# First attention's last head: 48 products of the output projection between its steps, and the places and engines of the work around them

## The chip, the cores and the metric

One core of one Trainium2 chip runs the whole program. The core has five engines with a program each: TensorE (PE, matrix products and transposes), VectorE (DVE), ScalarE (ACT), GpSimd (POOL), and SyncE (SP), whose queue starts the transfers between device memory and the core's memory. An engine takes its instructions strictly in order and waits at one until the semaphores named in the code have reached their counts. The metric is the time of one execution on the device in microseconds (us); lower is better.

## The reference

Two layers on an input of 1024 rows by 1024 columns, all in float32, so the sums must be good to float32. Layer 0 is differential attention and an MLP; layer 1 is a sliding window attention and an MLP. The change is at the end of layer 0's attention:

```python
h = rms_norm(x, attn_norm_g[0])
q, k, v = h @ w_qkv                       # 8 heads; q and k in two halves of 64, v of 128
p = softmax(q_c @ k_c.T - slope*distance) # for c = 0 and 1, chunk-causal mask
o = (p[0] - lam * p[1]) @ v               # one 1024x128 block for each head
o = rms_norm(o, subln_g) * (1 - lambda_init)
x = x + concat(o of 8 heads) @ w_o        # w_o: 1024x1024
x = x + relu(rms_norm(x, mlp_norm_g[0]) @ w_up)**2 @ w_down
```

## The kernel before

**Numbers.** A float32 value is held as a high part (rounded by ScalarE with a copy) and a low part (VectorE: value minus high part, the function `low`). A product of two such values is three matrix products: high by high, high by low, low by high. For a block of the attention's output these parts are `a_hi[:, c]` and `a_lo[:, c]`, c being the head (a "chunk" of 128 rows of w_o), each 128 partitions by 1024. A panel of w_o is 128 of its columns, with its parts `w_hi[i]` and `w_lo[i]`, which lie in the memory of `w_op`; so the traces call them w_op.

**The attention.** Heads run in a pipeline over 8 blocks of queries (steps s = 0 to 7). For each step TensorE makes the scores, VectorE takes their maxima (`maxima`, `both_maxima`), ScalarE the exponentials (`exps`), VectorE mixes the two softmaxes (`mix`), TensorE transposes the mixed weights (`transpose_weights`), ScalarE and VectorE split them (`high_wT`, `low_wT`), and TensorE multiplies them with the values (`values`, one step behind). In heads 0 to 6 the projection of the next head's q, k and v fills TensorE between these steps. The last head (head 7, `last_head` on each engine) has no next head: its steps hold only its own scores, transposes and values.

A head's output is divided by its root mean square ("norm"): VectorE makes a first guess of the inverse root from the sums of squares (`o_factors`), three Newton steps refine it, a product applies it to the head's block, and TensorE transposes the result (`transpose_outputs`). ScalarE copies that out (`evac_o`, to `xT`, called oT here) and makes `a_hi` (`high_early`), VectorE `a_lo`. For heads 0 to 6 the Newton steps and the product are GpSimd's (its `head`, lines 866 to 884: 13 small instructions and one of 128x1024). For head 7 they are VectorE's, `rsqrt_steps_dve` and the product, right behind the last values.

**The output projection.** It follows in `segment(0)` of each engine. Eight panels, two halves of 512 rows each, in three pairs of PSUM banks in turn, `wo_bank[0]`: score0 and score1 hold two banks each, and proj and pv one each. A panel is 8 chunks by 2 halves by 3 = 48 products of 128x512. Panels 0 and 1 begin early: behind the last values TensorE makes their products with `a_hi` of chunks 0 to 6, then those with `a_lo`, and transposes the outputs of head 7 between them. VectorE adds each half to the residual (`add_x`, result `xs`), which needs the residual's tile, loaded from device memory by SyncE (`load_unit`: four tiles of 128x512 for each two panels, a "unit"). ScalarE multiplies `xs` with the norm's gain and squares it, GpSimd sums the squares (`ss`) and makes sums and differences of the unit's tiles for the MLP (`minus`), which uses seven products of sub-blocks for each eight. VectorE splits the units' seven operands (`xop`). A panel's weights are loaded by SyncE (`load_wo`, two places `w_raw` in the memory of `w_quad`), and split by ScalarE and VectorE (`split_panel`), panels 0 and 1 in the last head's steps 5 and 6, panel 2 behind head 7's norm, and each later one two panels ahead, in the loop of the segment. SyncE loads the second unit only when `a_lo` of all eight chunks is there.

**The order of work** is written out by hand, engine by engine. No planner and no cost table takes part: each engine's instructions run in the order in which the functions write them.

## Time and profile before

| | |
|---|---|
| time, median of 3 runs | 2198.53 us (2195.86 to 2199.34) |
| the profiled execution's own time | 2196.21 us |
| its span in the trace | 2194.5 us |
| granted TensorE clock, mean of the span | 0.991 of full speed |
| TensorE busy | 2143.5 us, 98% of the span, 11580 products and transposes |
| VectorE busy | 1566.1 us, 71% |
| ScalarE busy | 1137.7 us, 52% |
| GpSimd busy | 761.1 us, 35% |
| chain that ended last, by engine | PE 82%, DVE 10%, issue 4%, ACT 2% |

The time is that of the whole execution on the device; the span is the stretch that the trace covers, 1.7 us shorter. Busy is the time in which an engine ran an instruction. The clock is the share of its full speed that TensorE was granted. The stretch that the change touches is short: the last head from 469.8 to 518.0 us, the projection's eight panels from there to 606.

### The profile page before, as it was taken

To read this page: it belongs to the slowest core of one execution; us is meant where nothing else is said; L and a number is where in the kernel's file an instruction comes from. 1 tells how busy PE (TensorE), PEld (TensorE's weight loads), DVE (VectorE), ACT (ScalarE), POOL (GpSimd) and SP (SyncE) were. 2 spreads that over 40 slices of the span, in tenths; PEclk is the share of its full clock that TensorE was granted. 3 is DMA by queue.
4 is the path that set the end of the run, shared out by engine and by line. 5 is a ranking of instruction groups with operands and counts; after the bars stand their busy time and mean duration, and the time that the engine had idled before them with its cause. 6 is when DMAs were issued, how large, how long until landed. Compare 5 with 4: busy or idle time off the path is not lost.

```text
span 2194.5 us, 34725 instructions
## 1 busy us (share of the span) xinstructions
PE 2143.5 (98%) x11580; PEld 1843.0 (84%) x11580; DVE 1566.1 (71%) x3011; ACT 1137.7 (52%) x2429; POOL 761.1 (35%) x1200
## 2 busy tenths in 40 slices
PE   7999999998999999999999999999999999999999
PEld 6999999987888888788888899988888888788887
DVE  6788788887586666778767757775766666886783
ACT  5566566655455455624434446764555555443342
POOL 3334333331642222333225225435622222322331
PEclk9999999989999999999999999999999999999999
DMA  6111110003424444754534111105244445654252
GB/s 207 42 30 30 29 29 23 1 20 106 135 87 158 158 158 143 262 185 164 192 131 157 62 53 48 29 11 173 92 158 158 152 141 209 251 192 151 99 184 84
DMA packets 190916, 257.71 MB, mean 117 GB/s; under 512 B 15136, under 2 KB 139552, under 8 KB 186144
## 3 DMA queue, kind: packets, MB, share of 16 engines
q1 hardware_dynamic: 190752, 255.65, 35.0%
q8 instruction: 87, 1.43, 0.3%
q14 instruction: 77, 0.63, 0.1%
HBM read 174.09 MB, written 79.69 MB: 116 GB/s over the span
## 4 chain that ended last, share of the span: by engine, by line
PE 82%; DVE 10%; issue 4%; ACT 2%; POOLq 0%; DVEq 0%; DMA 0%; POOL 0%; ACTq 0%; SPq 0%
PE score L2193 42%; PE proj L2193 15%; PE trb L2193 14%; PE pv L2193 6%; DVE xop L1548 4%; DVE w_op L1548 2%; DVE xT L1868 1%; PE trb L2236 1%; ACT p L1119 1%; PE trb L2290 1%; PE trb L2611 1%; DVE p L1735 0%; PE score L2598 0%; DMA xop<-u_dram 0%; PE trb L2264 0%
## 5 line engine op out<-in xcount | busy, mean ns | idle before, releaser
L2193 PE MATMUL score<-xop,w_op 128*128 128x512 f32 x3840 | 892.5, 391 | 6.5 <-DVE xT L1868 5.7
L2193 PEld LDWEIGHTS score<-xop,w_op 128*128 128x128 f32 x3840 | 723.4, 189 | 160.4 <-issue 10.2
L2193 PE MATMUL trb<-xop,w_op 128*128 128x512 f32 x1536 | 362.0, 391 | 5.3 <-DVE xT L1868 4.6
L897 POOL TENSOR_TENSOR w_quad<-w_quad,w_sum 128x512 f32<-128x512 f32 x64 | 83.7, 1308 | 782.6 <-DVE w_op L1548 782.6
L2193 PEld LDWEIGHTS trb<-xop,w_op 128*128 128x128 f32 x1536 | 287.5, 188 | 68.7 <-DVE w_op L1548 7.4
L1041 ACT ACTIVATE w_op<-w_quad 128x512 fp32r<-128x512 f32 (+1 forms) x336 | 214.0, 644 | 228.1 <-PE score L2193 109.3
L1548 DVE TENSOR_TENSOR w_op<-w_quad,w_op 128x512 fp32r<-128x512 f32 (+1 forms) x335 | 293.1, 880 | 41.0 <-ACT w_op L1041 41.0
L1868 DVE TENSOR_TENSOR xT<-score,xT 128x512 f32<-128x512 f32 x160 | 109.0, 686 | 138.8 <-PE score L2193 133.1
L1548 DVE TENSOR_TENSOR xop<-xop 128x1024 fp32r<-128x1024 f32 x112 | 150.9, 1365 | 3.7 <-ACT xop L1041 3.7
L1041 ACT ACTIVATE quad<-score 128x512 f32<-128x512 f32 x96 | 57.2, 596 | 176.4 <-PE score L2193 174.1
L1041 ACT ACTIVATE xop<-xop 128x1024 fp32r<-128x1024 f32 x112 | 117.0, 1053 | 56.1 <-DMA xop<-u_dram 55.2
L2193 PE MATMUL proj<-wa_hi,a_hi 128*128 128x384 f32 x418 | 142.5, 341 | 0.9 <-DVE v_parts L1549 0.9
L1119 ACT ACTIVATE p<-p,nm_a,slopes 128x128 f32<-128x128 f32 (+7 forms) x112 | 96.4, 863 | 90.3 <-DVE nm_a L1740 90.3
L2193 PE MATMUL proj<-wa_hi,a_lo 128*128 128x384 f32 x418 | 139.9, 335 | 0.0
L2193 PE MATMUL proj<-wa_lo,a_hi 128*128 128x384 f32 x418 | 139.8, 334 | 0.0
L1868 DVE TENSOR_TENSOR quad<-trb,quad 128x512 f32<-128x512 f32 x64 | 44.2, 690 | 110.1 <-PE trb L2193 75.3
L1041 ACT ACTIVATE w_op<-w_sum 128x512 fp32r<-128x512 f32 x128 | 76.9, 625 | 81.1 <-PE trb L2193 33.2
L2193 PE MATMUL score<-a_hi,w_op 128*128 128x512 f32 x368 | 110.3, 391 | 0.1
L519 POOL TENSOR_TENSOR chain_p<-rstd_qk 128x8 f32<-128x8 f32 x96 | 19.1, 199 | 244.6 <-DVE rstd_qk L511 235.3
L897 POOL TENSOR_TENSOR w_quad<-w_quad 128x512 f32<-128x512 f32 x64 | 100.6, 1573 | 5.0
L1735 DVE CUSTOM_DVE_ANT_0 p<-score,dist_a 128x128 f32<-128x128 f32 (+7 forms) x112 | 80.3, 754 | 29.8 <-PE score L2193 29.8
L911 POOL TENSOR_TENSOR w_sum<-w_quad 128x512 f32<-128x512 f32 x64 | 89.2, 1394 | 31.2 <-DMA w_quad<-in_mlp_w_down 24.1
(320 smaller groups left out, 4285.4 us busy)
## 6 DMA issues: line engine op xcount, KB each, us to landing
xop<-u_dram SPq DMA_DIRECT2D x112, 512.0 KB, 5.0
u_dram<-quad SPq DMA_DIRECT2D x32, 1536.0 KB, 9.5
w_quad<-in_mlp_w_up SPq DMA_DIRECT2D x64, 512.0 KB, 5.4
w_quad<-in_mlp_w_down SPq DMA_DIRECT2D x64, 512.0 KB, 4.9
wa_raw<-in_a_w_qkv SPq DMA_DIRECT2D x96, 128.0 KB, 2.5
quad<-xT_dram SPq DMA_DIRECT2D x32, 256.0 KB, 3.8
xT_dram<-xs SPq DMA_DIRECT2D x32, 256.0 KB, 2.4
u_dram<-quad SPq DMA_DIRECT2D x32, 256.0 KB, 3.5
```

Of the source, the lines that this page charges most:

```text
L519: eng.tensor_tensor(t, out, out, ALU.mult)
L897: return pool.tensor_tensor(out, x, y, ALU.subtract)
L911: pool.tensor_tensor(w_full(n, "S1"), quarter(n, 1, 0), quarter(n, 1, 1), ALU.add)\
L1041: return nc.scalar.activation(out, in_, ACT.Copy, scale=scale)
L1119: nc.scalar.activation(p[:, 0:keys], p[:, 0:keys], ACT.Exp, bias=nm_a[i][:, c:c + 1], scale=one(slopes, h), accum_out=ssum[par][:, c, s:s ...
L1548: return nc.vector.tensor_tensor(out, full, hi.bitcast(F32), ALU.subtract)
L1735: nc.vector.tensor_tensor_reduce(out=p[:, 0:keys], in0=score[c][:, 0:keys], in1=dist_a[:, S - keys:S], scale=1.0, scalar=LOWEST, op0=ALU.a ...
L1868: return nc.vector.tensor_tensor(out, a, b, ALU.add)
L2193: return nc.tensor.matmul(out, a, b, start=start, stop=stop, **kw)
L2236: last = nc.tensor.transpose(trb[b][:, P * (kc - 4 * i):P * (kc - 4 * i + 1)], p0[block_s % 2][:, P * kc:P * (kc + 1)], ident[:, :])
L2290: last = nc.tensor.transpose(trb[b][:, P * i:P * (i + 1)], qk2[:, (s - 3) % 4 + i % 2, P * (i // 2):P * (i // 2 + 1)], ident[:, :])
L2611: last = nc.tensor.transpose(trb[b][0:P - lo, P * u:P * (u + 1)], pb[:, e, r, lo:P], ident[:, :])
```

## The change

Eight parts, in the order of the program.

1. The panels are split in the order 2, 0, 1, 3 and so on (`SPLIT_ORDER`). Panel 2's weights get a place of their own (`raw2`), are loaded behind the attention's own last weights and split in head 6, step 2. Panel 0's high part is made after the last head's first exponentials, its low part moves from VectorE to GpSimd, in four pieces of 128x256. Panel 3 gets a place of its own (`w_op` slot 4 and `w_low3`) and is split right behind the last head.
2. `a_hi` of chunks 0 to 3 is made at the last head's start, of 4 and 5 in step 1.
3. TensorE makes 36 products of `a_hi` of chunks 0 to 5 with both parts of the weights (`panel_high`) between the steps of the last head, into the bank proj, which the attention no longer uses: 12 each for panel 2's second half, panel 0's first and panel 0's second. ScalarE copies each finished sum out (`keep`, to `kept`, 128x512). 12 more, panel 2's first half, stand behind the last transposes and ahead of the last values, in the bank where they stay.
4. GpSimd adds the three kept sums to the residual's tiles before VectorE adds the rest: two when the norm is done, and the third behind `clear()`, when the second unit is loaded and ahead of its first difference and sums of squares. `add_x` waits for these three.
5. Behind the last values TensorE makes 24 products of panel 1, 12 of chunk 6 for three panels, 18 with `a_lo` of chunks 0 to 2, the transposes of head 7, and 24 with `a_lo` of chunks 3 to 6; then chunk 7 of the three panels (18) and panel 3.
6. The norm of head 7 moves from VectorE to GpSimd, its product in four pieces of 128x256; head 6's product is in four pieces as well. VectorE makes `a_lo` of chunks 0 and 1 ahead of head 7's guess and the others behind it.
7. VectorE's guess for head 6 moves from step 2 to step 1, behind the maxima.
8. Some semaphores are merged (`lam_steps`, `passed`), with the same order of work.

```diff
+LATE = 6
+SPLIT_ORDER = (2, 0, 1, 3, 4, 5, 6, 7)
...
+        scope = ExitStack()
+        kept = [sb(f"kept{i}", [P, HALF], F32, scope) for i in range(3)]
...
+        raw2 = sb("raw2", [P, KC, P], F32, scope)
+        w_raw2 = raw2[:, :, :]
...
+        w_low3 = sb("w_low3", [P, KC, P], F32R, scope)
...
+            if i == 3 and not seg:
+                return w_op[:, 4, :, :].rearrange("p a (k n) -> p (a k) n", n=P), w_low3[:, :, :]
...
+        def split_count(seg, panel):
+
+            return KC * seg + (panel if seg else SPLIT_ORDER.index(panel)) + 1
...
+            sp.wait_ge(wa_lo_done, NH * 4)
+            sp.dma_start(w_raw2, w_out[0].rearrange("(k p) n -> p k n", p=P)[:, :, 2 * P:3 * P])\
+                .then_inc(w_in[0], 16)
...
                         sp.wait_ge(w_lo_done, KC * seg + i - 1)
+                    elif i == 3:
+                        sp.wait_ge(w_lo_done, split_count(0, 1))
...
-            run_heads(pool, head)
+            def norm_outputs(done, o):
+
+                pool.wait_ge(o_rstd, done)
+                norm_steps(rstd_o[:, :], chain_o, NB)
+                for b in range(0, NB, 2):
+                    last = pool.tensor_tensor(o[:, b:b + 2, :], o[:, b:b + 2, :],
+                                              rstd_o[:, b:b + 2].unsqueeze(2).to_broadcast([P, 2, P]), ALU.mult)
+                last.then_inc(o_normed, 1)
+
+            def last_head():
+
+                pool.wait_ge(w_lo_done, split_count(0, 2))
+                pool.wait_ge(w_hi_done, split_count(0, 0))
+                for k in range(0, KC, 2):
+                    last = pool.tensor_tensor(w_lo[0][:, k:k + 2, :], w_raw[0][:, k:k + 2, :],
+                                              w_hi[0][:, k:k + 2, :].bitcast(F32), ALU.subtract)
+                last.then_inc(w_lo_done, 1)
+                norm_outputs(NH - 1, head_out[0])
+                norm_outputs(NH, head_out[1])
+
...
+                    for i, (panel, half) in enumerate(((2, 1), (0, 0), (0, 1))):
+                        if panel:
+                            continue
+                        pool.wait_ge(half_kept, i + 1)
+                        pool.wait_ge(quad_in[0], 64)
+                        x = quad[0][:, TILE[0, half], :]
+                        pool.tensor_tensor(x, x, kept[i][:, :], ALU.add).then_inc(half_added, 1)
...
+                if seg == 0:
+                    pool.wait_ge(quad_in[1], 64)
+                    x = quad[1][:, TILE[0, 1], :]
+                    pool.tensor_tensor(x, x, kept[0][:, :], ALU.add).then_inc(half_added, 1)
...
+                act.wait_ge(w_in[i % 2], panel // 2 * 16 + (16 if panel else 32))
...
+                    act.wait_ge(mixed, NH * NB)
...
+                def keep(i):
+                    act.wait_ge(half_ready, i + 1)
+                    copy(kept[i][:, :], proj[:, :]).then_inc(half_kept, 1)
+
                 act.wait_ge(qkv_ready, NH * NB)
+                high_early(0)
+                high_early(1)
                 last_exps(0)
                 high_wT(uses, 0)
+                split_panel(0)
+                high_early(2)
...
                 for s in range(NB - 1):
 
...
                         act.drain()
                         square_outputs(h * 4, 1 - par, 6)
                     if s == 1:
-                        high_early(0)
...
                     if s == 2:
+                        keep(0)
...
-                    if s >= 4:
-                        high_early(s - 3)
+                    if s == 4:
+                        keep(1)
                     if s in (4, 5):
                         act.drain()
...
+                    if s == 5:
+                        split_panel(1)
+                    if s == 6:
+                        keep(2)
                 act.drain()
                 square_outputs(h * 4 + 3, par, 4)
...
+                        act.wait_ge(w_in[0], 16)
+                        copy(w_hi[2], w_raw2).then_inc(w_hi_done, 1)
...
+            split_panel(3)
...
                     if s == 0:
                         row_sums(h - 1, NB - 1)
-                    if s == 2:
-                        o_factors(h, 1 - par)
-                    if s == NB - 1:
-                        split_panel(0)
...
+                    if s == 1:
+                        o_factors(h, 1 - par)
...
+                dve.wait_ge(w_lo_done, split_count(0, 0))
                 split_panel(1)
...
+            low_outputs_a(0, 2)
             take_outputs(NH * NB - 1, 1, NB - 2)
             o_factors(NH, 1)
-            dve.wait_ge(o_normed, NH - 1)
-            dve.drain()
-            rsqrt_steps_dve(nc.vector, rstd_o[:, :], chain_o, chain_p, NB)
...
-            nc.vector.tensor_tensor(head_out[1], head_out[1],
...
+            low_outputs_a(2, EARLY[0])
+            split_panel(3)
...
+                        if seg == 0 and (i, half) in ((0, 0), (0, 1), (2, 1)):
+                            dve.wait_ge(half_added, i + half + 1 if i == 0 else 3)
...
+                pe.wait_ge(qkv_free, NH * NB)
+                pe.wait_ge(w_lo_done, split_count(0, 2))
+                panel_high(proj[:, :], 2, 1, (0, 1))
                 values(uses, 0, NB - 1, h * 4 - 1, 1 - par)
+                panel_high(proj[:, :], 2, 1, (2,))
...
+                    if s == 0:
+                        panel_high(proj[:, :], 2, 1, (3,))
+                    if s == 2:
+                        panel_high(proj[:, :], 2, 1, (4, 5)).then_inc(half_ready, 1)
+                    if s == 3:
+                        pe.wait_ge(half_kept, 1)
+                        pe.wait_ge(w_lo_done, split_count(0, 0))
+                        panel_high(proj[:, :], 0, 0, (0, 1, 2))
+                    if s == 4:
+                        panel_high(proj[:, :], 0, 0, (3, 4, 5)).then_inc(half_ready, 1)
+                    if s == 5:
+                        pe.wait_ge(half_kept, 2)
+                        panel_high(proj[:, :], 0, 1, (0, 1, 2))
+                    if s == 6:
+                        panel_high(proj[:, :], 0, 1, (3, 4, 5)).then_inc(half_ready, 1)
                     if s + 2 < NB:
...
+            pe.wait_ge(score_max, 2 * NH * NB)
+            pe.wait_ge(half_kept, 3)
+            panel_high(wo_bank[0][2][0], 2, 0, range(LATE))
             values(last_uses, 0, NB - 1, NH * 4 - 1, 1)
...
-                        x_h = a_hi[:, k, HALF * i:HALF * (i + 1)]
-                        mm(wo_bank[0][slot][i], w_hi[slot][:, k, :], x_h, k == 0, False)
-                        mm(wo_bank[0][slot][i], w_lo[slot][:, k, :], x_h, False, False)
-                    if slot and k == 2:
-                        transpose_outputs(last_uses, NH, 1)
-            for slot in range(2):
-                for k in range(EARLY[0]):
-                    pe.wait_ge(o_split, k + 1)
-                    for i in range(2):
-                        mm(wo_bank[0][slot][i], w_hi[slot][:, k, :], a_lo[:, k, HALF * i:HALF * (i + 1)], False, False)
+            pe.wait_ge(w_lo_done, split_count(0, 1))
+            for half in range(2):
+                panel_high(wo_bank[0][1][half], 1, half, range(LATE))
+            pe.wait_ge(pv_free, NH * 4)
+            for panel in range(3):
+                for half in range(2):
+                    panel_high(wo_bank[0][panel][half], panel, half, range(LATE, EARLY[0]))
+            for c in range(3):
+                panel_lows(c)
+            transpose_outputs(last_uses, NH, 1)
+            for c in range(3, EARLY[0]):
+                panel_lows(c)
```

`panel_high` and `panel_lows` are new and called above:

```diff
+            def panel_high(out, panel, half, chunks):
+
+                for c in chunks:
+                    pe.wait_ge(o_early_hi, c + 1)
+                    x_h = a_hi[:, c, HALF * half:HALF * (half + 1)]
+                    kept_half = (panel, half) in ((2, 1), (0, 0), (0, 1))
+                    mm(out, w_hi[panel][:, c, :], x_h, c == 0 or kept_half and c == LATE, False)
+                    last = mm(out, w_lo[panel][:, c, :], x_h, False, kept_half and c == LATE - 1)
+                return last
+
+            def panel_lows(c):
+
+                pe.wait_ge(o_split, c + 1)
+                for panel in range(3):
+                    for half in range(2):
+                        mm(wo_bank[0][panel][half], w_hi[panel][:, c, :], a_lo[:, c, HALF * half:HALF * (half + 1)], False, False)
```

**The order before and after.** First TensorE, from the values of the last head's step 5 to the segment. Names: p_0 and p_1 are the mixed weights of even and odd steps, ident is the identity of a transpose, oraw the output of head 7; score, proj and pv are PSUM banks. Before, in two pieces, around the last transposes and behind the last values:

```order
L2193 MATMUL pv<-v_parts,wT_lo 128x256
L2193 MATMUL pv<-v_parts,wT_hi 128x256
L2193 MATMUL pv<-v_parts,wT_lo 128x256
L2236 MATMUL trb<-ident,p_1 128x128 x8
L2193 MATMUL pv<-v_parts,wT_hi 128x256
L2193 MATMUL pv<-v_parts,wT_lo 128x256
L2193 MATMUL pv<-v_parts,wT_hi 128x256
```

```order
L2193 MATMUL pv<-v_parts,wT_hi 128x256
L2193 MATMUL pv<-v_parts,wT_lo 128x256
L2193 MATMUL score<-a_hi,w_op 128x512 x40
L2264 MATMUL trb<-ident,oraw 128x128 x8
L2193 MATMUL score<-a_hi,w_op 128x512 x16
L2193 MATMUL score<-a_lo,w_op 128x512 x28
L2193 MATMUL score<-a_hi,w_op 128x512
```

After, the same two places:

```order
L2266 MATMUL pv<-v_parts,wT_hi 128x256
L2266 MATMUL pv<-v_parts,wT_lo 128x256
L2309 MATMUL trb<-ident,p_1 128x128 x8
L2266 MATMUL proj<-a_hi,w_op 128x512 x12
L2266 MATMUL pv<-v_parts,wT_hi 128x256
L2266 MATMUL pv<-v_parts,wT_lo 128x256
```

```order
L2266 MATMUL score<-a_hi,w_op 128x512 x32
L2266 MATMUL proj<-a_hi,w_op 128x512 x2
L2266 MATMUL pv<-a_hi,w_op 128x512 x2
L2266 MATMUL score<-a_lo,w_op 128x512 x4
L2266 MATMUL proj<-a_lo,w_op 128x512
L2266 MATMUL pv<-a_lo,w_op 128x512
```

and, three rows of the same kind later:

```order
L2266 MATMUL score<-a_lo,w_op 128x512 x4
L2266 MATMUL proj<-a_lo,w_op 128x512
L2266 MATMUL pv<-a_lo,w_op 128x512
L2337 MATMUL trb<-ident,oraw 128x128 x8
L2266 MATMUL score<-a_lo,w_op 128x512 x4
```

Twelve products stand between the last transposes and the last values (the proj row of the first piece after); of the earlier steps, steps 0 and 2 to 6 have two, four or six there. Behind the last values the 40 products with `a_hi` ahead of the transposes of oraw have become 36, and 18 with `a_lo` have come in, so that 54 stand ahead of these transposes instead of 40.

VectorE behind the last values' split, before:

```order
L1548 TENSOR_TENSOR wT_lo<-trb,wT_hi 128x512 x2
L1822 TENSOR_REDUCE oraw<-pv 128x256
L1831 TENSOR_TENSOR s0sq<-ssum 128x8
L1832 TENSOR_SCALAR chain_o<-oss 128x8
L1834 SCALAR_TENSOR_TENSOR chain_o<-s0sq,chain_o 128x8
L509 TENSOR_SCALAR chain_s<-chain_o 128x8
L511 TENSOR_SCALAR rstd_o<-chain_s 128x8
L536 SCALAR_TENSOR_TENSOR chain_p<-chain_o,rstd_o 128x8
L538 TENSOR_TENSOR chain_p<-chain_p,rstd_o 128x8
```

And after:

```order
L1619 TENSOR_TENSOR a_lo<-xT,a_hi 128x1024 x2
L1895 TENSOR_REDUCE oraw<-pv 128x256
L1904 TENSOR_TENSOR s0sq<-ssum 128x8
L1905 TENSOR_SCALAR chain_o<-oss 128x8
L1907 SCALAR_TENSOR_TENSOR chain_o<-s0sq,chain_o 128x8
L529 TENSOR_SCALAR chain_s<-chain_o 128x8
L531 TENSOR_SCALAR rstd_o<-chain_s 128x8
L1619 TENSOR_TENSOR a_lo<-xT,a_hi 128x1024 x5
L1619 TENSOR_TENSOR w_low<-w_quad,w_op 128x1024
L1619 TENSOR_TENSOR a_lo<-xT,a_hi 128x1024
L1939 TENSOR_TENSOR xs<-score,quad 128x512 x4
L1619 TENSOR_TENSOR w_op<-w_quad,w_op 128x1024
```

The guess (the row L531, before L511) is no longer followed by the Newton steps (L536 to L540, three of each) and the product L1853; the splits of `a_lo` follow at once.

GpSimd, from head 6's product (`xT`) on. Before:

```order
L880 TENSOR_TENSOR xT<-xT,rstd_o 128x1024
L889 MEMSET ss 128x512 x2
L897 TENSOR_TENSOR quad<-quad 128x512
L894 TENSOR_TENSOR ss<-ss,quad 128x512 x4
L897 TENSOR_TENSOR quad<-quad 128x512 x4
```

After, from the end of head 7's Newton steps (their first 11 rows left out):

```order
L545 TENSOR_SCALAR chain_p<-chain_p 128x8
L547 TENSOR_TENSOR rstd_o<-rstd_o,chain_p 128x8
L912 TENSOR_TENSOR oraw<-oraw,rstd_o 128x256 x4
L949 TENSOR_TENSOR quad<-quad,kept 128x512 x2
L932 MEMSET ss 128x512 x2
L957 TENSOR_TENSOR quad<-quad,kept 128x512
L940 TENSOR_TENSOR quad<-quad 128x512
L937 TENSOR_TENSOR ss<-ss,quad 128x512 x4
L940 TENSOR_TENSOR quad<-quad 128x512 x4
```

Head 7's Newton steps and product, and the three additions of `kept`, now stand ahead of the first sum of the unit (`quad<-quad`) and of the squares (`ss<-ss,quad`).

## Rows read from the trace of the kernel before

**Rows 1.** Stretches: start:end, length, busy time (count) by engine, clock, DMA share, GB/s.

```profile
469.80:518.00 48.20, 34.88 (x218) 28.30 (x218) 39.41 (x107) 32.86 (x78) 9.11 (x28) 0.82 0.15 42
476.00:478.00 2.00, 1.88 (x10) 1.53 (x11) 1.88 (x8) 0.54 (x2) 1.15 (x6) 0.55 0.00 0
488.00:490.00 2.00, 2.00 (x12) 2.00 (x12) 1.93 (x7) 0.00 (x0) 1.90 (x1) 0.54 0.00 0
```

**Rows 2.** TensorE's waits in 469.8:518: who waited <- for whom, us in all, times, longest.

```profile
PE pv L2193 <- DVE wT_lo L1548: 8.0, 4, 3.6
PE score L2193 <- DVE mx_a L1775: 3.9, 4, 1.5
```

**Rows 3.** Timeline of TensorE: start, us, instruction, count, idle before it <- who ended it.

```profile
474.67 0.35 PE L2193 MATMUL pv<-v_parts,wT_hi 128*128 128x256 f32 x1 [2.15 <-DVE wT_lo L1548]
...
516.00 0.36 PE L2193 MATMUL pv<-v_parts,wT_hi 128*128 128x256 f32 x1 [1.67 <-DVE wT_lo L1548]
...
518.00 9.26 PE L2193 MATMUL score<-a_hi,w_op 128*128 128x512 f32 x40
527.10 1.03 PE L2264 MATMUL trb<-ident,oraw 128*128 128x128 f32 x8
```

**Rows 4.** Timeline of VectorE behind the last values.

```profile
520.47 0.17 DVE L511 TENSOR_SCALAR rstd_o<-chain_s 128x8 int32<-128x8 int32 x1
...
524.07 8.03 DVE L1548 TENSOR_TENSOR a_lo<-xT,a_hi 128x1024 fp32r<-128x1024 f32 x7
...
533.15 1.22 DVE L1548 TENSOR_TENSOR a_lo<-xT,a_hi 128x1024 fp32r<-128x1024 f32 x1
```

**Rows 5.** Timeline of GpSimd: head 6's Newton steps begin, and their product.

```profile
482.78 0.20 POOL L519 TENSOR_TENSOR chain_p<-rstd_o 128x8 f32<-128x8 f32 x1 [1.55 <-DVE rstd_o L511]
...
487.54 2.36 POOL L880 TENSOR_TENSOR xT<-xT,rstd_o 128x1024 f32<-128x1024 f32 x1
```

**Rows 6.** Timeline of VectorE at two places where GpSimd is busy.

```profile
39.43 1.23 DVE L1568 CUSTOM_DVE_ANT_0 x_junk<-x_tok 128x1024 f32<-128x1024 f32 x1
...
423.19 0.93 DVE L1749 SCALAR_TENSOR_TENSOR coef_a<-ssum,neg_lam,rcp_a 128x1 f32<-128x1 f32 x1
```

**Rows 7.** Timeline of GpSimd at the same two places.

```profile
39.51 1.21 POOL L523 TENSOR_TENSOR chain_p<-chain_p 128x8 f32<-128x8 f32 x1
...
423.06 1.05 POOL L873 TENSOR_TENSOR qk<-qk,rstd_qk 128x512 f32<-128x512 f32 x1
```

**Rows 8.** Timeline of ScalarE: head 7's output copied out and split; two squares.

```profile
527.73 1.27 ACT L1041 ACTIVATE xT<-trb,gsub 128x512 f32<-128x512 f32 x2 [6.22 <-PE trb L2264]
529.09 1.06 ACT L1041 ACTIVATE a_hi<-xT 128x1024 fp32r<-128x1024 f32 x1
...
547.41 1.14 ACT L1277 ACTIVATE quad<-xs 128x512 f32<-128x512 f32 x2
```

**Rows 9.** SyncE's loads of the second unit, and their landing.

```profile
535.38 2.32 SPq L670 DMA_DIRECT2D quad<-xT_dram  x4
...
DMA to landing us min/median/max: 5.6/5.9/7.4
```

**Rows 10.** Timeline of VectorE in the panels; last row GpSimd.

```profile
549.53 2.20 DVE L1548 TENSOR_TENSOR w_op<-w_quad,w_op 128x1024 fp32r<-128x1024 f32 x1 [2.78 <-ACT w_op L1041]
...
572.85 1.37 DVE L1868 TENSOR_TENSOR xs<-score,quad 128x512 f32<-128x512 f32 x2 [2.61 <-PE score L2193]
...
599.92 2.38 DVE L1548 TENSOR_TENSOR w_op<-w_sum,w_op 128x512 fp32r<-128x512 f32 x2
...
602.82 0.68 DVE L1868 TENSOR_TENSOR xs<-score,quad 128x512 f32<-128x512 f32 x1
604.82 3.07 DVE L1548 TENSOR_TENSOR xop<-quad,xop 128x512 fp32r<-128x512 f32 x2 [1.31 <-ACT xop L1041]
...
595.64 1.29 POOL L897 TENSOR_TENSOR w_sum<-w_sum,w_quad 128x512 f32<-128x512 f32 x1
```

**Rows 11.** Chain that ended last, the piece before the first MLP products.

```profile
584.37 24.53 PE score L2193 x108
```

## What the change will do to the time

> **What bounds the kernel now.** First the page's part 1: TensorE is busy 98% of the span, so on the whole only what shortens TensorE's own list or fills its gaps can help. Then the busy time by stretches: the last head is the exception. In its 48.20 us TensorE is busy 34.88, so 13.3 us are idle, and its mean clock is 0.82 [rows 1]. The waits say for whom: 8.0 us for VectorE's splits of the transposed weights ahead of the values, 3.9 us for maxima ahead of scores [rows 2]. The timeline shows where: a wait of 2.15 us ahead of 474.67, one of 1.67 us ahead of 516.00, one of 3.6 between [rows 2, 3]. Behind 518.00 TensorE has none: 40 products take until 527.10, 0.2275 us each (9.10/40) [rows 3]. Call the end of the last values T: 518.0 before. From there to the first MLP product all 384 products of the eight panels run on the critical chain; its last piece, 96 of them and 12 of the MLP, starts at 584.37 [rows 11], so the MLP begins at about 584.37 + 96 x 0.2275 = 606.2.
>
> The last view is VectorE in the panels. It is less idle than its 71% say. It splits panel 4 at 549.53 (call this D), waits 2.61 us for TensorE at 572.85, and makes the last half of panel 7 at 602.82; the first operand that is waited for in the MLP comes out of 604.82 [rows 10]. So a second chain, VectorE with ScalarE and GpSimd, runs just behind TensorE, and the saving is limited by the one that shrinks less.
>
> **TensorE's side.** 48 products leave the stretch behind T: 48 x 0.2275 = 10.9 us. Of these 36 go into the idle 13.3 us of the last head: at full clock 8.2 us of work, in groups of 2 to 6 (0.5 to 1.4 us), each ahead of values that wait for VectorE in any case. The last 12 take 2.73 us at full clock where 1.67 us of waiting stood [rows 3], so T moves by +1.06, to about 519.1. Below this: if the groups keep the clock up, the transposes and values at the end get quicker, and T may be 517.4. Above: 520 to 521, where ScalarE's three copies to `kept` (the nearest row is 0.6 us for a 128x512) or GpSimd's pieces hold VectorE. The extra copy and split in head 6 I cost at nothing, since there the projection of the next head keeps TensorE busy; without that cover they are 1.06 + 1.15 [rows 4, 8], an end of the range. If nothing else is late the saving is 10.9 − 1.1 = 9.8 us.
>
> **The chain behind T on the other engines** (times after T). VectorE's guess ends at 520.47 + 0.17 = T + 2.64 [rows 4]; the two splits ahead of it in the order lie under the last 12 products. Now the norm is GpSimd's. In head 6, 13 Newton steps there took 487.54 − 482.78 = 4.76 us, and the product 2.36 [rows 5]. VectorE had both done 3.43 us after its guess (524.07 − 520.64) [rows 4], T + 6.1; so even alone the move costs 3.7 us: norm at T + 9.8. But at once behind the guess VectorE makes seven splits of 1.15 us (8.03/7) [rows 4], each reading two operands, while GpSimd makes small steps. What then happens is in two places of the trace. A VectorE instruction of 1.23 us and a GpSimd step of 128x8, which took 0.20 [rows 5] elsewhere, overlap: GpSimd's takes 1.21. A GpSimd product of 1.05 us and a 128x1 of VectorE: VectorE's takes 0.93, ending with GpSimd's [rows 6, 7]. So the later one waits until the earlier has ended, in both directions. With every gap between splits used by one step, six steps cost 1.15 + 0.2 = 1.35 each, 8.1 us; the other seven 0.37 (4.76/13), 2.6; the product about 2.0: norm at 2.64 + 8.1 + 2.6 + 2.0 = T + 15.3. I take this, and 9.8 as the other end.
>
> The Trainium skill has this rule (SBUF — State Buffer, "Who interferes with whom"): a VectorE instruction with two inputs in SBUF and a GpSimd one that reads SBUF share a port pair under an exclusive lock, taken by whichever issues first, and the other fully blocks. The 1.21 against 0.20 agrees. A sharing of throughput instead of a lock would leave the norm near T + 9.8.
>
> TensorE reaches the transposes after 54 products, at T + 12.3 (before: after 40). It waits there 3.0 us, which only eats part of the 9.8. From transposes (527.10) to the end of `a_hi` (529.09 + 1.06) are 3.05 us [rows 3, 8], and the split 1.15: `a_lo` of chunk 7 at T + 19.5. SyncE issues the second unit's loads only behind that: from 534.37 (533.15 + 1.22) [rows 4] to the last issue, 535.38 + 2.32, are 3.3 us, and each lands 5.6 to 7.4 us after its issue [rows 9]: T + 28.4. Before, nothing early depended on it. Now GpSimd waits for it in order to add the third kept sum, and queued behind are its first difference and the squares of panel 0. ScalarE's squares of panel 1 write the tiles that these read, and behind them stands its copy for panel 4. So: addition 1.3 and difference 1.3 (as the 1.29 of 595.64 [rows 10]), two squares 2.5, ScalarE's square 0.57 (1.14/2) [rows 8], copy 1.06, handoffs 0.3: D = T + 28.4 + 7.0 = T + 35.4. Before D was T + 31.5. With T = 519.1, D = 554.5, 5.0 us later than before.
>
> **How much of that is hidden.** From D to 602.82 VectorE's chain has the 2.61 us wait for TensorE; at the end the GpSimd sums are ready at 596.93 and VectorE reads them at 599.92 with a copy of 0.6 and handoffs of 0.3 between, 2.1 us to spare. So the chain needs 53.3 − 4.7 = 48.6 us from D. The first MLP operand that VectorE makes late is ready at 605.5 (604.82 + 0.68) and is needed after six products, 606.2 + 1.4 = 607.6: another 2.0. Together 6.7 of cover against 5.0 lost: **saving 1.7 us**. The third addition in itself, the two others (TensorE still has panel 3 to do) and the merged semaphores add nothing more. Panel 3's split right behind the last head is made before D and so takes 2.2 us of ScalarE and VectorE from the loop; I count that as filling VectorE's wait, worth 0 to 1.
>
> **The sum.** The profiled execution took 2196.2 us of its own: 2196.2 − 1.7 = 2194.5. The median of the three runs is 2.3 above it: 2196.8. I predict 2196.5, as the small terms lean to the good side.
>
> **The rivals.**
> *A: GpSimd's norm is not held up.* For it: its steps are 0.20 us and VectorE's instructions have handoffs between them. Against: 1.21 us in rows 7. The norm is at T + 9.8, TensorE arrives at T + 12.3 without waiting, the chain is 3.0 us shorter, the saving 1.7 + 3.0 = 4.7: 2193.8.
> *B: TensorE bounds all through.* For it: 98% busy, and the chain shows only TensorE in rows 11. Then VectorE's margins are larger than I read them, or loads land sooner, and the whole 9.8 us come in, with up to 0.7 of gaps: 2198.5 − 10.5 = 2188.
> *C, slower: the last head's products run at half clock.* Behind the wait of 2.15 us the clock was 0.55 from 476 to 478 and still 0.54 at 488 to 490, and there TensorE was busy 94 to 100% [rows 1, 3]. A product at half clock costs 0.455 (twice 0.2275). If the clock stays low between 490 and 512 too, the 22 products of steps 2 to 5 take 10 us instead of 5, without cover, since all else of TensorE doubles as well; T = 519 + 5 + about 1 for VectorE's guess behind it = 524.5 to 525. D moves with it, 10.5 us later than before against 6.7 of cover: 4 slower, about 2202.5. It decides if the granted clock from 490 to 506 is nearer to 0.5 than to 1.0. Against it: the clock fell behind that wait, and the products shorten the waits.
>
> **Chances.** The forecast 0.48, its own range 2193.5 to 2199.5; A 0.18; B 0.20; C 0.14. Differences under 0.2% (4.4 us) can't be told from none: under 2194.1 is faster, over 2202.9 slower. B is all faster, A about half, the forecast 0.06 of its 0.48: 0.35. C is about half slower, and a little of the forecast: 0.13. The rest is 0.52. The range reaches from 2187 (B with T at 517.4) to 2202.5.
>
> **What would show it.** In the changed kernel's trace: T between 518 and 521; the last head's clock; GpSimd's steps for head 7 at over 1 us each next to VectorE's splits, and a wait of TensorE of about 3 us ahead of its transposes; GpSimd waiting for the second unit's load until T + 28 with ScalarE's copy for panel 4 waiting behind it; split of panel 4 at about 554.5; the MLP starting at about 604.5. A start of the MLP before 598 shows B; T over 523 shows C. I am wrong if VectorE's split of panel 4 is early and yet nothing is gained, or if TensorE waits in a place not named here.

## The result, and the profile after

The changed kernel is slower: 2202.14 us, median of 16 runs (2197.95 to 2203.74), against 2198.48 us for the kernel before (16 runs, 2195.41 to 2203.51). The ratio is 1.0014, 95% interval 1.0007 to 1.0020: 3.1 us lost, 1.5 to 4.4. That is under the 0.2% named in the prediction, and on the other side of what it forecast, 2 us faster.

The two traces have to be laid over each other first: the profiled execution of the changed kernel is the slowest of its sixteen (2203.74 us), that of the kernel before is on the fast side (2196.21). Their spans differ by 6.3 us, and the first 2.07 us of this are there before anything that the change touches: head 6's last seven transposes start at 462.63 in the kernel before and at 464.70 in the changed one. TensorE's timeline and the stretch of 44 to 47 us show where most of it, 1.6 us, comes from, the kernel before first:

```profile
43.71 0.65 PE L2290 MATMUL trb<-ident,qk 128*128 128x128 f32 x4 [2.26 <-POOL qk L873]
...
44.00:47.00 3.00, 3.00 (x21) 3.00 (x20) 2.81 (x9) 0.80 (x3) 0.00 (x0) 1.00 0.39 141
```

and the changed kernel, in the same place of the program:

```profile
44.08 0.34 PE L2363 MATMUL trb<-ident,qk 128*128 128x128 f32 x1 [2.25 <-POOL qk L896]
...
44.00:47.00 3.00, 2.92 (x11) 2.92 (x12) 2.89 (x8) 1.16 (x3) 0.02 (x1) 0.54 0.26 97
```

Both wait 2.25 us for the same norm; behind it one execution goes on at full clock and the other at 0.54 for three microseconds. The work is the same there. So I measure from T0, the start of those seven transposes, and write T, D and the rest against it.

| us after T0 | before | after |
|---|---|---|
| end of the last values, T | 55.4 | 58.2 |
| split of panel 4 on VectorE, D | 86.9 | 93.5 |
| MLP's seventh product on TensorE (first operand made late) | 144.7 | 146.7 |
| first sums of squares on TensorE | 154.3 | 159.5 |
| spread of the row factors on TensorE | 169.0 | 172.2 |

The sums of squares are TensorE's products of `ones` and `ss`, the spread its next products of `ss` and `ones`. The last line leaves 3.2 us, close to the 3.1 of the medians; from there to the end the two spans differ by another 1.0, which was not followed. (The seventh product before is 605.97 + 6 x 0.2275.) What TensorE waited for in the changed kernel, from the last head on (columns as in [rows 2]):

```profile
PE pv L2266 <- DVE wT_lo L1619: 5.4, 3, 2.2
PE score L2266 <- DVE xop L1619: 4.7, 1, 4.7
PE trb L2337 <- POOL oraw L912: 2.1, 1, 2.1
PE score L2266 <- DVE w_op L1619: 1.2, 1, 1.2
PE proj L2266 <- DVE w_op L1619: 1.1, 1, 1.1
...
PE score L2266 <- DVE mx_a L1849: 0.8, 1, 0.8
```

The waits of the last head have shrunk from 8.0 and 3.9 us to 5.4 and 0.8 [rows 2]: the products do fill them. But four waits of 9.1 us stand where there was none. TensorE's own list became 10.9 us shorter behind T (48 x 0.2275), and it waits for most of that. Its timeline at these places:

```profile
513.99 0.35 PE L2266 MATMUL pv<-v_parts,wT_hi 128*128 128x256 f32 x1 [2.18 <-DVE wT_lo L1619]
...
516.07 1.91 PE L2309 MATMUL trb<-ident,p 128*128 128x128 f32 x8
517.63 3.51 PE L2266 MATMUL proj<-a_hi,w_op 128*128 128x512 f32 x12
...
522.89 7.44 PE L2266 MATMUL score<-a_hi,w_op 128*128 128x512 f32 x32
...
537.44 1.10 PE L2337 MATMUL trb<-ident,oraw 128*128 128x128 f32 x8 [2.12 <-POOL oraw L912]
...
605.23 1.52 PE L2266 MATMUL score<-xop,w_op 128*128 128x512 f32 x6
611.42 3.34 PE L2266 MATMUL score<-xop,w_op 128*128 128x512 f32 x6 [4.67 <-DVE xop L1619]
614.55 4.38 PE L2266 MATMUL trb<-xop,w_op 128*128 128x512 f32 x12
```

The 54 products end 12.4 us behind 522.89, and the transposes of head 7 then wait 2.12 us. The MLP's first six products take 1.52 us; then comes the wait of 4.67 us, and behind it six take 3.34 and twelve 4.38 (twelve took 2.93 and twelve 2.91 before, from 605.97 on). The stretches show the clock there, and in the last head (columns as in [rows 1]):

```profile
469.80:522.90 53.10, 45.09 (x284) 36.09 (x283) 43.98 (x111) 37.60 (x89) 12.26 (x35) 0.90 0.11 31
...
488.00:490.00 2.00, 2.00 (x7) 1.22 (x5) 1.59 (x7) 1.53 (x4) 1.21 (x6) 0.50 0.01 4
516.00:518.00 2.00, 2.00 (x11) 2.00 (x10) 0.96 (x2) 0.60 (x1) 0.00 (x0) 0.50 0.02 6
612.00:614.00 2.00, 1.95 (x5) 1.13 (x4) 2.00 (x3) 0.58 (x2) 0.51 (x1) 0.50 0.00 0
```

TensorE is busy all or nearly all of 488 to 490, 516 to 518 and 612 to 614 and gets half of its clock, each time behind a wait of 2.2 to 4.7 us.

**The chain.** GpSimd's norm of head 7 and third addition, VectorE, and ScalarE ahead of panel 4:

```profile
525.62 1.11 POOL L539 TENSOR_TENSOR chain_p<-rstd_o 128x8 f32<-128x8 f32 x1 [31.93 <-DVE rstd_o L531]
...
531.41 1.00 POOL L539 TENSOR_TENSOR chain_p<-rstd_o 128x8 f32<-128x8 f32 x1
532.55 0.20 POOL L543 TENSOR_TENSOR chain_p<-chain_p 128x8 f32<-128x8 f32 x1
...
535.06 2.32 POOL L912 TENSOR_TENSOR oraw<-oraw,rstd_o 128x256 f32<-128x256 f32 x4
...
551.46 1.29 POOL L957 TENSOR_TENSOR quad<-quad,kept 128x512 f32<-128x512 f32 x1 [10.66 <-DMA quad<-xT_dram]
```

```profile
525.45 5.77 DVE L1619 TENSOR_TENSOR a_lo<-xT,a_hi 128x1024 fp32r<-128x1024 f32 x5
...
540.66 1.23 DVE L1619 TENSOR_TENSOR a_lo<-xT,a_hi 128x1024 fp32r<-128x1024 f32 x1 [8.30 <-ACT a_hi L1096]
...
552.26 1.37 DVE L1939 TENSOR_TENSOR xs<-score,quad 128x512 f32<-128x512 f32 x2 [6.17 <-DMA xT_dram<-xs]
558.16 1.93 DVE L1619 TENSOR_TENSOR w_op<-w_quad,w_op 128x1024 fp32r<-128x1024 f32 x1 [4.53 <-ACT w_op L1096]
...
610.01 3.04 DVE L1619 TENSOR_TENSOR xop<-quad,xop 128x512 fp32r<-128x512 f32 x2 [1.31 <-ACT xop L1096]
```

```profile
555.29 0.63 ACT L1348 ACTIVATE quad<-xs 128x512 f32<-128x512 f32 x1 [0.91 <-POOL ss L937]
...
557.08 1.04 ACT L1096 ACTIVATE w_op<-w_quad 128x1024 fp32r<-128x1024 f32 x1
```

GpSimd's first six steps take 0.7 to 1.2 us beside VectorE's six splits of 1.15, those behind them 0.20. The norm ends at 537.4, T + 14.5. GpSimd then waits for the second unit's load, adds the third kept sum at 551.46, and its difference and squares, for which ScalarE waits, come only behind that. D is 558.16, T + 35.3.

**The last head.** GpSimd's four pieces of panel 0 run from 483.26 to 486.05, and VectorE's guess for head 6, now in step 1, falls exactly there:

```profile
483.26 2.79 POOL L921 TENSOR_TENSOR w_op<-w_quad,w_op 128x256 fp32r<-128x256 f32 x4
```

```profile
483.44 0.58 DVE L1904 TENSOR_TENSOR s0sq<-ssum 128x8 f32<-128x8 f32 x1
...
485.48 0.61 DVE L531 TENSOR_SCALAR rstd_o<-chain_s 128x8 int32<-128x8 int32 x1
486.00 0.41 DVE L1619 TENSOR_TENSOR wT_lo<-trb,wT_hi 128x256 fp32r<-128x256 f32 x1
```

Its five instructions span 2.65 us; such a guess spanned about 1.0 in the kernel before (0.17 each [rows 4]). The split of the transposed weights (486.00) stands behind, and the third transposes are at T0 + 22.8 instead of 21.2. The last transposes are 1.1 us late (T0 + 51.4 instead of 50.2), T 2.8.

### The profile page after: what moved, and what is told of

The parts are those of the page before. It is cut to its first block and busy times, and to the rows that moved or that the text cites. A ratio compares the mean times of both kernels' runs of the same rounds, so it can differ in the third digit from the quotient of the medians.

```text
span 2200.8 us, 34754 instructions
## 1 busy us (share of the span) xinstructions
PE 2140.2 (97%) x11580; PEld 1836.8 (83%) x11580; DVE 1568.0 (71%) x3000; ACT 1138.7 (52%) x2432; POOL 780.3 (35%) x1227
## 5 line engine op out<-in xcount | busy, mean ns | idle before, releaser
L1096 ACT ACTIVATE quad<-score 128x512 f32<-128x512 f32 x96 | 57.2, 596 | 176.2 <-PE score L2266 173.8
L1096 ACT ACTIVATE xop<-xop 128x1024 fp32r<-128x1024 f32 x112 | 116.9, 1053 | 58.6 <-DMA xop<-u_dram 58.2
L1096 ACT ACTIVATE w_op<-w_sum 128x512 fp32r<-128x512 f32 x128 | 77.0, 625 | 85.6 <-PE trb L2266 32.7
L2266 PE MATMUL score<-a_hi,w_op 128*128 128x512 f32 x328 | 101.1, 392 | 1.3 <-DVE w_op L1619 1.2
```

Source lines behind the costliest of these rows:

```text
L1096: return nc.scalar.activation(out, in_, ACT.Copy, scale=scale)
L2266: return nc.tensor.matmul(out, a, b, start=start, stop=stop, **kw)
```

## The experiments

All are the changed kernel with an edit, but for one that is the kernel before. Ratios are to the kernel before, with 95% intervals; the last columns are from each trace. "MLP wait" is TensorE's wait ahead of the MLP's seventh product, "sums" the first sums of squares on TensorE.

| run | ratio | T - T0 | D - T0 | MLP wait | sums - T0 |
|---|---|---|---|---|---|
| before | 1 | 55.4 | 86.9 | none | 154.3 |
| changed kernel | 1.0014 (1.0007 to 1.0020) | 58.2 | 93.5 | 4.7 | 159.5 |
| GpSimd's panel 0 behind head 6's norm | 1.0019 (1.0009 to 1.0028) | 59.4 | 95.0 | 4.6 | 160.2 |
| products behind the scores | 1.0024 (1.0015 to 1.0033) | 59.7 | 95.4 | 4.6 | 162.1 |
| norm of head 7 on VectorE | 0.9998 (0.9989 to 1.0007) | 58.5 | 91.2 | 4.7 | 157.0 |
| third addition behind the squares | 1.0001 (0.9992 to 1.0010) | 56.6 | 90.1 | 4.4 | 156.4 |
| the last two together | 0.9993 (0.9984 to 1.0001) | 58.1 | 90.1 | 4.7 | 156.2 |
| GpSimd's panel 0 ahead of the queries' norm | 1.0007 (0.9999 to 1.0016) | 58.1 | 93.5 | 4.7 | 159.6 |
| four edits, transposes behind 36 products | 0.9979 (0.9970 to 0.9988) | 57.9 | 86.0 | 3.1 | 152.3 |
| sixteen products more | 1.0011 (1.0003 to 1.0020) | 58.0 | 93.1 | 2.5 | 157.7 |
| before, sixteen products more | 1.0019 (1.0010 to 1.0029) | 57.2 | 88.3 | none | 159.8 |
| twelve products behind the last values | 1.0011 (1.0002 to 1.0020) | 56.1 | 91.6 | 4.7 | 157.4 |
| four edits and these twelve | 0.9991 (0.9982 to 1.0000) | 56.7 | 86.6 | 3.1 | 153.3 |
| four edits without the third | 0.9983 (0.9972 to 0.9993) | 57.8 | 85.7 | 3.1 | 152.4 |

**1. Is it VectorE's chain or TensorE's list that binds?** Sixteen products are added ahead of panel 4, into a bank that the panel then starts anew, in both kernels:

```diff
+                    if i == 4 and seg == 0:
+                        for n in range(16):
+                            mm(wo_bank[0][1][n % 2], w_hi[1][:, 0, :], a_hi[:, 0, HALF * (n % 2):HALF * (n % 2 + 1)], True, True)
```

For the changed kernel:

> The changed kernel with 16 more products of 128x512 (3.64 us of TensorE) ahead of panel 4, into a bank that is started anew, so that the result is the same. If VectorE's chain sets the time there (TensorE waits 4.7 us for the first late operand of the MLP): the time stays within 0.7 us of the changed kernel's and that wait shrinks to about 1. If TensorE is what binds: 3.6 us more.

For the kernel before:

> The kernel before with the same 16 added products (3.64 us of TensorE) ahead of panel 4; the counterpart of the same addition to the changed kernel, which cost nothing (1.0011 against 1.0014). If TensorE is what binds before (its list is without a gap from T to the MLP): 2.5 to 3.6 us more, 1.0011 to 1.0016. If VectorE's chain binds there as well, within 1 us of the kernel before.

The same 3.64 us of TensorE cost the kernel before 4.2 us (1.0019, a little over what I expected) and the changed one nothing that can be told (1.0011 against 1.0014; the two intervals leave room for 2 us, not for 3.6). The changed kernel's row of the MLP wait, with the sixteen in it:

```profile
609.15 3.34 PE L2266 MATMUL score<-xop,w_op 128*128 128x512 f32 x6 [2.47 <-DVE xop L1619]
612.29 2.96 PE L2266 MATMUL trb<-xop,w_op 128*128 128x512 f32 x12
```

The wait went from 4.67 to 2.47 only, since other waits took up the rest; it did not end at 1 as I had written. The twelve behind it are at 2.96 instead of 4.38: behind the shorter wait the low clock lasts less in this trace. TensorE bound before and does not bind now: this is shown.

**2. Who makes D late?** The norm of head 7 goes back to VectorE:

```diff
-                norm_outputs(NH, head_out[1])
...
             o_factors(NH, 1)
+            dve.wait_ge(o_normed, NH - 1)
+            dve.drain()
+            rsqrt_steps_dve(nc.vector, rstd_o[:, :], chain_o, chain_p, NB)
+            dve.drain()
+            nc.vector.tensor_tensor(head_out[1], head_out[1],
+                                    rstd_o[:, :].unsqueeze(2).to_broadcast([P, NB, P]), ALU.mult).then_inc(o_normed, 1)
             low_outputs_a(2, EARLY[0])
```

> The changed kernel with one edit: head 7's Newton steps and product are VectorE's again, right behind its guess, ahead of the splits of chunks 2 to 6. If GpSimd's norm, held up by VectorE's splits, is what TensorE waited 2.1 us for: that wait is gone, TensorE reaches the transposes at T + 12.3, and the split of panel 4 (D) comes at T + 33.2 instead of T + 35.3; the time falls by 1.5 to 2, to 1.0006 of before. Rival: VectorE's 3.4 us put its own splits late by as much, chunk 7's low part comes no sooner, D stays at T + 35.3 and so does the time.

D came at T + 32.7 and TensorE's 2.12 us wait is gone; the rival is out. The ratio fell from 1.0014 to 0.9998, which is 3.5 us and more than expected; the two intervals allow 1.5 as well.

And the third addition goes behind the squares of panel 0:

```diff
-                if seg == 0:
-                    pool.wait_ge(quad_in[1], 64)
-                    x = quad[1][:, TILE[0, 1], :]
-                    pool.tensor_tensor(x, x, kept[0][:, :], ALU.add).then_inc(half_added, 1)
...
                             add_square(square_of(c, half), half, 36 * seg + 2 * c + half + 1)
+                    if c == 0 and seg == 0:
+                        pool.wait_ge(quad_in[1], 64)
+                        x = quad[1][:, TILE[0, 1], :]
+                        pool.tensor_tensor(x, x, kept[0][:, :], ALU.add).then_inc(half_added, 1)
```

> The changed kernel with one edit: GpSimd's addition of the third kept sum, which waits for the second unit's load, stands behind the unit's first difference and the squares of panel 0 instead of ahead of them. If that load holds ScalarE's squares of panel 1: D falls from T + 35.3 to about T + 33.7, limited then by the store of panel 0's sums, for which VectorE already waits 6.2 us, and the time by about 1.5. Rival: D is set by that store alone, and nothing changes (under 0.3).

D came at T + 33.5. GpSimd and VectorE there:

```profile
548.13 2.53 POOL L937 TENSOR_TENSOR ss<-ss,quad 128x512 f32<-128x512 f32 x2
550.62 1.30 POOL L989 TENSOR_TENSOR quad<-quad,kept 128x512 f32<-128x512 f32 x1
...
550.51 1.38 DVE L1938 TENSOR_TENSOR xs<-score,quad 128x512 f32<-128x512 f32 x2 [4.47 <-DMA xT_dram<-xs]
554.67 2.20 DVE L1618 TENSOR_TENSOR w_op<-w_quad,w_op 128x1024 fp32r<-128x1024 f32 x1 [2.79 <-ACT w_op L1095]
```

The squares no longer wait for the load, nor ScalarE for the squares; what is left ahead of D is VectorE's wait for the store of panel 0's sums (4.47 us) and the usual one for ScalarE's copy (2.79). The rival, that this store alone sets D, is out too. Part of this run's gain in the trace is luck: its T is 1.6 us earlier because the clock held (below).

Both together:

> The changed kernel with both edits that helped: head 7's norm on VectorE, and GpSimd's third addition behind the squares of panel 0. Each alone took 3 to 4 us off the median (0.9998 and 1.0001 of before against 1.0014). If D decides (the split of panel 4, found at T + 32.7 and T + 33.5 instead of T + 35.3) and the two sit one behind the other on its chain: D at T + 31.0, time about 1.5 us under the better of the two, 0.9991 of before. If they hide each other, D stays at T + 32.7 and the time at 0.9998.

D is T + 31.95, between the two answers. The ratio, 0.9993, lies where the first theory put it, but its interval touches both. More than half of the second gain is lost to the store: VectorE now waits 6.93 us for it.

**3. Who makes T late?** Theory 1 was GpSimd's pieces, which block VectorE; theory 2 the products ahead of the scores. The pieces behind head 6's norm (the six lines are moved as they are):

```diff
             def last_head():
+                norm_outputs(NH - 1, head_out[0])
                 pool.wait_ge(w_lo_done, split_count(0, 2))
...
-                norm_outputs(NH - 1, head_out[0])
```

> The changed kernel with one edit: GpSimd splits panel 0 (four pieces of 128x256) behind the norm of head 6 instead of ahead of it. T0 is the start of head 6's last seven transposes, T the end of the last values: T - T0 is 55.4 us in the kernel before, 58.2 in the changed one. Theory 1 (the pieces block VectorE's guess for head 6, which took 2.56 us instead of 1.0, and with it the last head's chain): the guess takes 1.0 to 1.2 us, T - T0 falls by about 1.5 to 56.7, the time to 1.0007 of before. Theory 2 (it is the products ahead of the scores that make VectorE's maxima late): T - T0 stays at 58.2. If panel 0's low part is now late for the products of step 3, TensorE waits there, up to 1 us.

```profile
484.00 0.16 DVE L1904 TENSOR_TENSOR s0sq<-ssum 128x8 f32<-128x8 f32 x1
...
484.81 0.17 DVE L531 TENSOR_SCALAR rstd_o<-chain_s 128x8 int32<-128x8 int32 x1
...
495.41 2.90 PE L2266 MATMUL proj<-a_hi,w_op 128*128 128x512 f32 x6 [3.66 <-issue]
```

The guess spans 1.0 us again, and the third transposes are at T0 + 21.2, as before the change: the first half of theory 1 holds. But T and the time, which were to fall to 56.7 and 1.0007, rose: panel 0's low part is late, TensorE stands 3.66 us for it (at most 1 was expected), and T is 1.2 later. The products behind the scores:

```diff
                     transpose_weights(uses, s + 1, s, h * NB + s)
+                    if s + 2 < NB:
+                        scores(h, s + 2, par)
                     if s == 0:
                         panel_high(proj[:, :], 2, 1, (3,))
...
-                    if s + 2 < NB:
-                        scores(h, s + 2, par)
                     values(uses, s + 1, s, h * 4 + s // 2, par)
```

> The changed kernel with one edit: in each step of the last head the projection's products stand behind the step's scores instead of ahead of them (36 products, same groups). Theory 2 (products ahead of the scores delay the maxima): T - T0 falls from 58.2 to about 56.5, time about 1.5 us less. Theory 1 (GpSimd's pieces): T - T0 within 0.5 of 58.2, or later where a group no longer fits into the wait ahead of the values.

Theory 2 falls: T is 1.5 later, at T0 + 59.7. TensorE now waits 3.6 us for maxima ahead of the scores and the products no longer stand in those waits. And the pieces ahead of the queries' norm (the same lines, in `head` of head 6 at step 7, ahead of `pool.wait_ge(qk_rstd, ...)`):

> The changed kernel with one edit: GpSimd splits panel 0 ahead of the norm of the last queries and keys, in time in which it waits, instead of behind it. If the block on VectorE's guess is what put the last head 1.5 us late (putting the pieces behind head 6's norm made the guess short, 1.0 us, but TensorE then waited 3.7 us for panel 0's low part): the guess takes 1.0, the third transposes start at T0 + 21.2 as before (22.8 in the changed kernel), T - T0 is 56.7, or 55.1 where the clock holds behind the 2.18 us wait. Time 1.5 less than the changed kernel's. If the queries' norm, now 2.8 us later, comes late for TensorE's transposes in step 2, nothing is gained.

```profile
475.39 0.67 DVE L1793 TENSOR_SCALAR chain_q<-stat_m,msq 128x4 f32<-128x4 f32 x1
...
476.83 0.62 DVE L531 TENSOR_SCALAR rstd_qk<-chain_s 128x8 int32<-128x8 int32 x1
```

T stays at 58.1. The pieces now block the guess for the queries: instructions of 128x4 and 128x8 take 0.62 to 0.67 us instead of 0.17 to 0.23. The block has moved, not gone: head 6's guess spans 1.4 us, but the third transposes are still at T0 + 22.8. So no run took the block away without something else in its place, and what it costs at T is not shown. Whether the 1.0007 is a gain can't be told.

The end of the last head is the other part. The twelve products behind the last values:

```diff
+            values(last_uses, 0, NB - 1, NH * 4 - 1, 1)
             pe.wait_ge(score_max, 2 * NH * NB)
             pe.wait_ge(half_kept, 3)
             panel_high(wo_bank[0][2][0], 2, 0, range(LATE))
-            values(last_uses, 0, NB - 1, NH * 4 - 1, 1)
```

> The changed kernel with one edit: the twelve products of panel 2's first half stand behind the last values instead of ahead of them. The norm of head 7, and all that follows from it, hangs on T. If the twelve put T late by their 2.7 to 3.5 us less the wait that they fill (1.7): T - T0 falls to 56.0 to 56.5, D with it by 1.7 to 2.2, time 1.5 to 2 us under the changed kernel's, 1.0006. Rival: TensorE reaches the transposes later after T by as much (T + 17.3), behind the norm, so D and the time stay.

T and D are 2.1 and 1.8 us earlier, as the first answer has it. The ratio, 1.0011 where 1.0006 was expected, can't be told from the changed kernel's 1.0014. In this run the clock held ahead of the last transposes, so 1.3 of the 2.1 us may be that. What the clock is worth there shows in two runs with the same program up to that place and the same wait, 2.18 us: the changed kernel's last transposes and twelve products took 1.91 and 3.51 us (above), and those of the run with the third addition behind the squares 1.04 and 2.99:

```profile
513.89 0.35 PE L2265 MATMUL pv<-v_parts,wT_hi 128*128 128x256 f32 x1 [2.18 <-DVE wT_lo L1618]
...
515.63 1.04 PE L2308 MATMUL trb<-ident,p 128*128 128x128 f32 x8
516.42 2.99 PE L2265 MATMUL proj<-a_hi,w_op 128*128 128x512 f32 x12
```

From the last transposes to T that run takes 5.5 us, this one 4.7: with the clock held in both, moving the twelve products makes T 0.8 us earlier.

**4. A version that beats both.** The two edits of part 2, GpSimd's pieces ahead of the queries' norm, and as a fourth TensorE's transposes of head 7 behind 36 products:

```diff
-            for c in range(3):
-                panel_lows(c)
             transpose_outputs(last_uses, NH, 1)
-            for c in range(3, EARLY[0]):
+            for c in range(EARLY[0]):
                 panel_lows(c)
```

> The changed kernel with four edits: norm of head 7 on VectorE, third addition behind the squares, GpSimd's split of panel 0 ahead of the queries' norm, and TensorE's transposes of head 7 behind 36 products instead of 54, so at T + 8.2. If the chain over VectorE decides: chunk 7's low part comes at about T + 12.4 (behind VectorE's other splits, T + 13), D at T + 28, T - T0 55 to 56.7, the MLP's first sum of squares on TensorE 4 to 6 us earlier than in the kernel before; time 0.9975 to 0.9985 of before. If TensorE's own list binds by then (it has 9.8 us less behind T than before), the gain ends at that.

```profile
531.82 1.03 PE L2341 MATMUL trb<-ident,oraw 128*128 128x128 f32 x8
...
536.50 1.21 DVE L1617 TENSOR_TENSOR a_lo<-xT,a_hi 128x1024 fp32r<-128x1024 f32 x1
...
551.73 2.24 DVE L1617 TENSOR_TENSOR w_op<-w_quad,w_op 128x1024 fp32r<-128x1024 f32 x1 [2.78 <-ACT w_op L1094]
...
605.33 3.33 PE L2270 MATMUL score<-xop,w_op 128*128 128x512 f32 x6 [3.09 <-DVE xop L1617]
```

2193.58 us against 2198.97, 0.9979 (0.9970 to 0.9988). The transposes are at T + 8.2, VectorE has chunk 7's low part at T + 14.1, D is T + 28.1. The transposes and D came as written, the low part 1 us later, and the time fell in the middle of its range. Two forecasts missed: T stayed at 57.9, outside 55 to 56.7, and the MLP's first sum of squares is 2.0 us earlier than in the kernel before, not 4 to 6. At the spread of the row factors it is 3.9 (T0 + 165.1 against 169.0); why the lead grows there is told below. With the twelve products behind the last values as a fifth edit:

> The version with four edits (0.9979 of before) and, as a fifth, the twelve products of panel 2's first half behind the last values. There TensorE's list is nearer to binding: it waits 3.1 us for the MLP's operands, but reaches the transposes at T + 10.9 instead of T + 8.2. If T falls by 1.7 to 2 and the transposes come at the same absolute time: within 0.5 us of 0.9979. If the end of the norm still decides: 1 us better, 0.9974.

It is 0.9991, neither answer, and the two intervals (0.9982 to 1.0000 against 0.9970 to 0.9988) just overlap. T fell by 1.2 us only; the transposes come at T + 10.9 as written, so 1.5 us later than with four edits, D is 0.6 us later and the MLP 1 us. That fits TensorE's list ahead of the transposes counting there. And without the third edit:

> The version with four edits without one of them: GpSimd's split of panel 0 is back behind the norm of the last queries and keys. By itself that edit moved the collision from VectorE's guess for head 6 (2.56 us to 1.4) to its guess for the queries (four small instructions of 0.17 to 0.23 us took 0.54 to 0.67), and T - T0 stayed at 58.1. So I expect no difference: 0.9975 to 0.9983 of before. If it mattered after all: 1 us slower, 0.9984 or more.

0.9983, D and the MLP within 0.3 us of the four edits'. No gain from the third edit can be told.

## Why the prediction was wrong

The mechanism was the one forecast, VectorE's chain behind D, but the forecast said that 6.7 us of cover would take the 5.0 us that it lost, and the kernel became slower. The 2202.1 us lie outside the forecast's own range of 2193.5 to 2199.5; that they are close to rival C's 2202.5 is chance, since C's cause did not come. By its own steps:

- **T behind the last values, +1.06: failed, +2.8.** This is the first of three terms that failed. 1.1 us of it are there at the last transposes. They begin with GpSimd's pieces on VectorE's guess for head 6, which put the third transposes 1.6 us late; how much of this reaches T is not shown, and ScalarE's three copies to `kept`, which the prediction named as well, were not tested. The prediction had the block in both directions from [rows 6, 7] and used it for head 7's norm, but for the last head it named the pieces only as an upper end for T (520 to 521 on the old scale). The step to ask was where four pieces of 0.7 us land on GpSimd, which is busy with the queries' norm until 483.3, just when VectorE's five steps begin. The other 1.7 us come from the last transposes to T, where the changed kernel takes 6.8 us and the one before 5.1: the twelve products ran partly at half clock. In the run where the clock held it is 5.5, so the low clock is worth 1.3 us there (the kernel before had a part of it too, its eight last transposes took 1.47 us).
- **Norm of head 7 at T + 15.3: right,** 14.5; six steps held up, as counted (beside six splits, not the seven of the sum). The Trainium skill's rule (SBUF — State Buffer, "Who interferes with whom"), that the pair is locked for whole instructions, agrees: 0.95 to 1.20 for five of these six steps against 0.20. A norm that is not held up would have ended near T + 9.8.
- **Wait of TensorE at the transposes, 3.0: in the right place,** 2.12.
- **D at T + 35.4: right,** 35.3, with the load, the addition and the squares in the order described. The experiments bear out both causes: 2.5 us for the norm, 1.8 for the third addition.
- **Cover of 6.7 us: failed, 4.6.** This is the second. D was 6.6 us late against T0. By my sum the MLP's seventh product would have been on time; it was 2.0 late. From D to that operand VectorE needed 52.5 us (558.16 to 610.69), not the 51.3 of the sum (48.6 and 2.7 from 602.82 to 605.5), and the product started 0.7 us after the operand. The waits on the way changed as well. In the kernel before VectorE stood 9.41 us for TensorE in the last panels, which the sum didn't name; in the changed one it stands 5.23 us at this place for a store, and then 1.85 us, ahead of 605.32, for ScalarE's copy of a sum that GpSimd finishes at 604.63. So 7.1 of the 12.0 us that VectorE had waited for TensorE behind D (2.61 and 9.41) were taken up by other waits:

```profile
594.61 1.37 DVE L1868 TENSOR_TENSOR xs<-score,quad 128x512 f32<-128x512 f32 x2 [9.41 <-PE score L2193]
```

```profile
597.33 1.33 DVE L1939 TENSOR_TENSOR xs<-score,quad 128x512 f32<-128x512 f32 x2 [5.23 <-DMA xT_dram<-xs]
```

- **What that wait does to the clock: not in the sum at all.** This is the third, a term put at nothing. TensorE is early now and waits 4.67 us, and the 18 products behind take 7.35 us (611.42 to 618.77) instead of 4.1 at full clock: 3.2 us. Two microseconds of this come back by the spread of the row factors, and that is no merit of the change: behind the sums of squares the clock of the kernel before falls (0.51 from 621 to 623), and 36 products take 10.02 us where the changed kernel's take 8.47. The fall is in both traces of kernels that do not wait ahead of the MLP (10.03 us in the one with sixteen products more), and in none of the other twelve. The prediction had a row on this effect [rows 1, 3], and asked for it in the last head only (rival C). C itself, T at 524.5, did not come: the clock was full from 492 to 514. The 36 products, before and after:

```profile
618.99 10.02 PE L2193 MATMUL score<-xop,w_op 128*128 128x512 f32 x36 [0.22 <-issue]
```

```profile
625.91 8.47 PE L2266 MATMUL score<-xop,w_op 128*128 128x512 f32 x36
```

- **Rival A** (norm not held up) is out, **rival B** (TensorE binds all through) as well: sixteen products more cost nothing that can be told.

Put together from the stations of the two traces, from T0: 2.8 + 3.8 − 4.6 of real cover = 2.0 late at the seventh product, 3.2 for the clock, and 2.0 given back: 3.2 us slower. The 4.6 are what the other stations leave, not a measurement of their own.

The products between the steps need not be given up: with chunk 7's low part early enough, the kernel that holds them is 4.6 us (2.6 to 6.6) faster than the one before (how much of this the other edits would bring without them wasn't run). The change took 10.9 us of products off TensorE behind T, 8.1 net of the later T, and put 6.6 us (2.8 at T, 3.8 behind it) on a chain that had 4.6 of cover.

Left open: whether the last head can have its products without a later T (no version of it got T under T0 + 56.1, and in two of the three lowest the clock held ahead of the last transposes), why TensorE's clock falls behind a wait of 2.2 us in one execution and not in another, and why it falls behind the sums of squares only in the kernels that do not wait ahead of the MLP.

## What to carry to other kernels

When products are taken off the engine that binds, follow the next chain from its first wait to where it meets that engine again, with the load, the store and the small additions that the change hangs into it; test it by adding idle work to the first engine, which costs nothing if it no longer binds. Before a piece of work goes to GpSimd, see which instructions of VectorE stand beside it in time: one small step each way can wait for a whole large one. A wait of the matrix engine is dearer than its length, if the work behind it then runs at half clock.

## What the runs showed of the hardware that I had not expected

- The same piece of program with the same wait of 2.25 us for the same norm went on at a clock of 1.00 in one execution and 0.54 in another, a difference of 1.6 us. Over all fourteen traces T0 is 462.3 to 463.1 us in seven and 464.6 to 466.0 in seven, with nothing between. In the seven early ones the clock is full from 30 to 70 us; in the late ones it is 0.79 to 0.91 in some stretch of 8 to 18 us there. In the last head, too, the clock fell behind a 2.18 us wait in some runs and held in others (1.91 against 1.04 us for the same eight transposes). Part of a kernel's spread between runs, 2195 to 2204 us here, may be this.
- VectorE instructions of 128x8 with one tensor operand (the guess, 0.17 us) are blocked by GpSimd's 128x256 subtractions as well, 0.61 us; I had only seen it for larger ones or ones with more operands.
- Adding 3.64 us of products made the changed kernel's trace reach the sums of squares 1.8 us earlier, since the shorter wait cost less clock. At the spread of the row factors 0.5 us of this is left (T0 + 171.7 against 172.2).
